# Hybrid flow backbone on one core: the scans' chunk blocks inverted by 32-row tiles, feature work and routing steps placed elsewhere

## The reference, cut to what matters

```python
def step(state, inp):                      # one token, per head; forward and backward in time
    r_t, w_t, k_t, v_t, a_t, b_t = inp
    sa = jnp.einsum('bhvk,bhk->bhv', state, a_t)
    state = (state * w_t[:, :, None, :] + sa[..., None] * b_t[:, :, None, :]
             + v_t[..., None] * k_t[:, :, None, :])
    return state, jnp.einsum('bhvk,bhk->bhv', state, r_t)
...
logits = (h @ w_router).astype(jnp.float32)
top_logit, top_idx = lax.top_k(logits, TOP_K)
```

## Time and profile before

| | us |
|---|---|
| median of 3 runs (lowest, highest) | 2844.2 (2843.36, 2848.82) |
| the profiled execution's own time | 2841.97 |
| its span | 2840.2 |
| PE, PEld busy | 2741.2, 2270.1 |
| DVE, ACT busy | 1923.5, 1524.9 |

### The profile page before, as it was taken

How to read it: one execution, slowest core, us unless ns; L and a number is a source line. 1 busy time by engine, 2 the same in 40 slices (tenths; PEclk the granted TensorE clock), 3 DMA queues, 4 the chain that set the end, 5 groups by cost and what they waited for, 6 DMA issues and landing times.

```text
span 2840.2 us, 49672 instructions
## 1 busy us (share of the span) xinstructions
PE 2741.2 (97%) x19396; PEld 2270.1 (80%) x19396; DVE 1923.5 (68%) x2524; ACT 1524.9 (54%) x2045; POOL 0.2 (0%) x4
## 2 busy tenths in 40 slices
PE   7999999999999999899999989999999999999997
PEld 5787777887788888667878988888888888888886
DVE  3766575336322333676656669888898988889897
ACT  5534374223322222543446447777777777777775
POOL 0000000000000000000000000000000000000000
PEclk8999999999999999999999989999999999999998
DMA  6010373224222232201034439999999999999995
GB/s 272 2 47 31 107 267 111 96 100 160 75 104 92 101 123 100 75 1 47 31 134 164 179 153 357 349 346 365 353 360 358 357 348 346 365 353 361 358 357 205
DMA packets 79842, 575.81 MB, mean 203 GB/s; under 512 B 8896, under 2 KB 10176, under 8 KB 10176
## 3 DMA queue, kind: packets, MB, share of 16 engines
q1 hardware_dynamic: 78960, 568.49, 53.1%
q10 hardware_dynamic: 720, 4.99, 0.4%
HBM read 572.39 MB, written 1.05 MB: 202 GB/s over the span
## 4 chain that ended last, share of the span: by engine, by line
PE 90%; DVE 6%; ACT 2%; issue 1%; DMA 0%; DVEq 0%; SPq 0%; ACTq 0%
PE bank L503 88%; ACT arena L1431 1%; PE bank L1339 1%; PE bank L1139 1%; DVE arena L2305 1%; DVE weights_low L1995 1%; DMA xT<-xin 0%; ACT weights_high L1431 0%; PE bank L924 0%; DVE arena L1971 0%; ACT hT L1431 0%; DVE arena L2211 0%; ACT L1431 0%; DVE arena L2091 0%; ACT modT L1431 0%
## 5 line engine op out<-in xcount | busy, mean ns | idle before, releaser
L1431 ACT ACTIVATE weights_high<-ring 128x1024 fp32r<-128x1024 f32 (+1 forms) x366 | 508.8, 1398 | 292.2 <-PE bank L503 291.9
L1431 ACT ACTIVATE arena<-bank 128x256 f32<-128x256 f32 (+7 forms) x581 | 255.6, 455 | 760.7 <-PE bank L503 684.1
L1995 DVE TENSOR_TENSOR weights_low<-ring,weights_high 128x1024 fp32r<-128x1024 f32 x220 | 266.7, 1224 | 403.0 <-ACT weights_high L1431 402.9
L2515 DVE TENSOR_TENSOR weights_low<-ring,weights_high 128x2048 fp32r<-128x2048 f32 x146 | 334.6, 2291 | 69.4 <-ACT weights_high L1431 67.9
L503 PE MATMUL bank<-h_low,weights_high 128*128 128x512 f32 (+1 forms) x960 | 346.8, 361 | 0.0
L503 PE MATMUL bank<-arena 64*64 64x64 f32 (+6 forms) x5168 | 301.2, 246 | 22.5 <-DVE arena L2211 5.8
L503 PEld LDWEIGHTS bank<-arena 64*64 64x64 f32 (+3 forms) x5168 | 252.1, 145 | 48.6 <-issue 17.4
L503 PE MATMUL bank<-weights_high,tokens_high 128*128 128x512 f32 x684 | 271.9, 397 | 1.6 <-DVEq L2538 1.6
L503 PE MATMUL bank<-weights_high,tokens_low 128*128 128x512 f32 x684 | 267.1, 390 | 0.0
L2515 DVE TENSOR_TENSOR more_weights_low<-arena,weights_high 128x2048 fp32r<-128x2048 f32 x108 | 247.4, 2291 | 25.0 <-ACT weights_high L1431 24.8
L1431 ACT ACTIVATE weights_high<-arena 128x2048 fp32r<-128x2048 f32 x108 | 207.0, 1917 | 47.1 <-PE bank L503 47.1
(11 more groups left out here) (294 smaller groups left out, 5348.0 us busy)
## 6 DMA issues: line engine op xcount, KB each, us to landing
ring<-wstream SPq DMA_DIRECT2D x372, 1024.0 KB, 4.8
arena<-wstream SPq DMA_DIRECT2D x167, 1024.0 KB, 4.8
sm<-small ACTq DMA_DIRECT2D x2, 1568.0 KB, 10.4
xT<-xin SPq DMA_DIRECT2D x1, 2048.0 KB, 9.8
cn<-consts ACTq DMA_DIRECT2D x1, 1636.0 KB, 6.6
out<-hT SPq DMA_DIRECT2D x2, 512.0 KB, 3.0
vec<-vecs SPq DMA_DIRECT2D x1, 121.5 KB, 2.6
cn<-consts ACTq DMA_DIRECT2D x1, 66.0 KB, 2.7
```

The lines of the kernel that those rows point to most:

```text
L1431: return nc.scalar.activation(o, i, func, **kw)
L1995: step(vx.tensor_tensor(ring_low[:, u % RING, cols], ring[:, u % RING, cols], wh[:, j % 4, :].bitcast(F32), ALU.subtract), "weights low", j)
L2515: return vx.tensor_tensor(low, raw, moe_high(q).bitcast(F32), ALU.subtract)
```

## The change

In the scans the doubling works on 32-row tiles. A helper `near` takes the place of `four`: for each head, four products of 32x32 by 32 columns, one per 32-row tile. E is cut in two: what lies in the same 32 rows but not in the same 16 (EB, mask "cross"), and what couples the two 32-row tiles of a half. F4 is the inverse at 16 rows, H = I + EB F4, and FT = F4 H the (transposed) inverse at 32 rows; Z is the coupling product that gives G1 at 64 rows. Z2, G2 and the second product of F4's kind are gone; D8 becomes a VectorE addition instead of a ScalarE copy; u is now the sum in PSUM of what u1 gave and the coupling. `gram_inner` issues 32 products instead of 16.

```diff
-            def four(o, left, right):
+            def near(b, at, left, right):
                 for h in range(4):
-                    for s in range(2):
-                        ins = mm(o[rows(s), h * HD:(h + 1) * HD], left[rows(s), h, :], right[rows(s), h, :])
+                    for t in range(4):
+                        ins = mm(bank[b][blk(t), at + h * BLK:at + (h + 1) * BLK], left[blk(t), h, :], right[blk(t), h, :])
...
             def carry_u(l, m):
+                pe.wait_ge(*done("G1", l, m))
...
-                        for s in range(2):
...
+                        for lead, follow in leads(groups[m][0]):
+                            ins = nc.tensor.matmul(bank[6 + p][blk(follow), P + q * HD:P + (q + 1) * HD],
+                                                   G_of[m % 2][blk(lead), 2 * p + q, follow % 2 * BLK:follow % 2 * BLK + BLK],
+                                                   u1[blk(lead), p, q, :], start=False, stop=True, skip_group_check=True)
...
# TensorE, solve(l, n), only the products of the solve
-                four(bank[4][:, 0:256], DD[:, 1], DD[:, 0])
-                four(bank[4][:, 256:512], DD[:, 0], DD[:, 1]).then_inc(*tick(products, "D2 product", l, n))
+                near(5, 0, DT, D)
+                near(5, P, D, DT).then_inc(*tick(products, "D2 product", l, n))
...
-                four(bank[4], DD[:, 1], DD[:, 0]).then_inc(*tick(products, "D8 product", l, n))
-                four(bank[5], DD[:, 0], FG[:, 0]).then_inc(*tick(products, "F3 product", l, n))
+                near(5, 0, D4[:, 0], D4[:, 1]).then_inc(*tick(products, "D8 product", l, n))
+                near(4, 256, D4[:, 1], F).then_inc(*tick(products, "F3 product", l, n))
...
-                four(bank[4][:, 256:512], D8, FG[:, 0]).then_inc(*tick(products, "F4 product", l, n))
+                near(4, 256, D8, F)
+                near(4, 384, F, D8).then_inc(*tick(products, "F4 product", l, n))
...
+                pe.wait_ge(*done("F4", l, n))
+                near(5, 0, E16, F4[:, 1]).then_inc(*tick(products, "H product", l, n))
                 if n:
                     carry_state(l, n - 1)
-                pe.wait_ge(*done("F4", l, n))
-                four(bank[5][:, 0:256], EC[:, 0], FG[:, 0])
-                four(bank[5][:, 256:512], FG[:, 0], EC[:, 0]).then_inc(*tick(products, "Z product", l, n))
-                pe.wait_ge(*done("masked k", l, n, 1))
-                across(bank[3], second, FG[:, 0], EC[:, 1], second).then_inc(*tick(products, "FC product", l, n))
+                pe.wait_ge(*done("H", l, n))
+                near(4, 256, F4[:, 0], H).then_inc(*tick(products, "FT product", l, n))
                 if n:
                     carry_y(l, n - 1)
-                pe.wait_ge(*done("Z", l, n))
+                pe.wait_ge(*done("FT", l, n))
+                pe.wait_ge(*done("masked k", l, n, 1))
+                for h in range(4):
+                    for t in range(second.start // BLK, second.stop // BLK):
+                        ins = mm(bank[3][blk(t), h * HD:(h + 1) * HD], FT[blk(t), h, :], EC[blk(t), 1, h, :])
...
-                four(bank[0], DD[:, 0], DD[:, 1]).then_inc(*tick(products, "Z2 product", l, n))
+                for h in range(4):
+                    for lead, follow in leads(d):
+                        at = 256 + h * HD + follow % 2 * BLK
+                        ins = mm(bank[0][blk(lead), at:at + BLK], E[blk(follow), h, :], FT[blk(follow), h, :])
...
# VectorE, solve(l, n)
-                    add(l, n - 1, 1, 0, 256, "G2")
...
+                elif n < 4:
+                    rates(l, 1, n - 2)
+                add(l, n, 4, "F2")
...
-                add(l, n, 0, 4, 256, "F4")
+                dve.wait_ge(*done("D8 product", l, n))
+                step(vx.tensor_tensor(D8, bank[5][:, 0:P].rearrange("p (h t) -> p h t", h=4), mask("eye32", BLK), ALU.add),
+                     "D8", l, n)
                 mask_k(l, n, 1)
+                if n in (0, 4):
+                    vx.memset(bank[0][:, 256:512], 0.0)
+                dve.wait_ge(*done("H product", l, n))
+                step(vx.tensor_tensor(H, bank[5][:, 0:P].rearrange("p (h t) -> p h t", h=4), mask("eye32", BLK), ALU.add),
+                     "H", l, n)
...
-                    rates(l, 1, n - 2)
-                    hats(l, 1, n - 2)
+                    second_hats(l, n - 2)
...
# ScalarE, solve(n)
+                    if n in (1, 2):
+                        second_exps(n - 1, 0)
+                        second_exps(n - 1, 1)
+                    if n in (1, 2):
+                        second_exps(n - 1, 2)
+                    copy(F4, bank[4][:, 256:512].rearrange("p (k h t) -> p k h t", k=2, h=4), ("F4", "F4 product"), n)
...
+                    if n == 0:
+                        f(es[:, 2:3], V("eps"), ACT.Exp)
...
-                    if n in (1, 2):
-                        exps(1, n - 1)
```

```diff
-                for t in range(2):
-                    ins = mm(bank[1 + 6 * t][:, 0:8], hT[:, k, CTX + t * P:CTX + (t + 1) * P], router_w[:, k, :],
-                             k == 0, k == KD - 1)
+                g = k % 4
+                ins = mm(bank[1][32 * g:32 * g + 32, 0:LAT], router_w[:, k, :], hT[:, k, CTX:TOK], k < 4, k >= 4)
...
# ScalarE, squares(...)
+                f(nm[:, 3:4], V("eps"), ACT.Sqrt)
                 for k in range(KD):
...
-                    if k == KD - 2:
-                        f(es[:, 3:4], V("eps"), ACT.Sqrt)
...
# ScalarE, layer 1, ahead of modulate
+                if l:
+                    first_high(0)
                 modulate(l, 2, both if l == 0 else both[1:], "ffn" if l == 0 else None)
...
# VectorE
+            dve.wait_ge(*done("first high", 0))
+            rest(0)
             dve.wait_ge(*done("logits"))
...
# VectorE, expert_pass, first instructions
+                dve.wait_ge(*in_pass(i - 1, "next high", AHEAD - 1))
+                rest(AHEAD - 1).then_inc(*tick(e_vectors, "low", AHEAD - 1))
```

More of the change, by code:

```diff
@@ L852, in gram_across @@
                 ins.then_inc(*tick(products, "gram across", l, n))
-            def last_power(l, n):
-                pe.wait_ge(*done("Z2", l, n))
-                pe.wait_ge(*done("G1", l, n))
-                four(bank[0][:, 256:512], D2[:, 1], FG_of[n % 2][:, 1]).then_inc(*tick(products, "G2 product", l, n))
             def across_second(l, n):
                 first, second = ends(groups[n][0])
-                pe.wait_ge(*done("G2", l, n))
+                pe.wait_ge(*done("G1", l, n))
                 pe.wait_ge(*done("FC", l, n))
-                across(bank[3], first, FW[:, 0], FG_of[n % 2][:, 1], second).then_inc(*tick(products, "W product", l, n))
+                across(bank[3], first, FW[:, 0], G_of[n % 2], second).then_inc(*tick(products, "W product", l, n))
             def solve(l, n):
@@ L1296, in _ @@
                 ins.then_inc(*tick(products, "tokens turned", i))
+                if i == 0:
+                    pe.wait_ge(*done("logit rows kept"))
+                    for t in range(2):
+                        ins = mm(bank[7][:, t * 8:(t + 1) * 8], T(LOGIT_ROWS)[:, t * P:(t + 1) * P], C("sel8", 8))
+                    ins.then_inc(*tick(products, "logits"))
             pe.wait_ge(*done("picks"))
@@ L1537, in _, with first_high @@
             act.dma_start(router_w[:], router).then_inc(router_loaded, 16)
+            def first_high(q):
+                act.wait_ge(moe_loaded[q], 16)
+                f(moe_high(q), moe_slot(q)[0], ACT.Copy).then_inc(*tick(scalars, "first high", q))
             for l in range(DEPTH):
@@ L1649, in solve @@
                     _, second = ends(groups[n][0])
-                    copy(D2, both_kinds(4), ("D2", "D2 product"), n)
+                    copy(D2, kinds(5), ("D2", "D2 product"), n)
                     if n:
@@ L1853, in _ @@
                             hidden_high(k)
-            for q in range(AHEAD):
-                act.wait_ge(moe_loaded[q], 16)
-                f(moe_high(q), moe_slot(q)[0], ACT.Copy).then_inc(*tick(scalars, "first high", q))
+            act.wait_ge(*done("logit rows"))
+            f(T(LOGIT_ROWS)[:, 0:LAT], bank[1][:, 0:LAT], ACT.Copy).then_inc(*tick(scalars, "logit rows kept"))
             for i in range(4):
@@ L1860, in _ @@
                     .then_inc(*tick(scalars, "tokens kept", i))
+            for q in range(1, AHEAD):
+                first_high(q)
             act.wait_ge(*done("top two"))
@@ L2126, in hat_k, with second_hats @@
                 step(vx.tensor_tensor(kh(d, j), X(d, KDIR_, j), X(d, TMP_, j), ALU.mult), "hats", l, d, j)
[L2128 to L2133 removed]
+            def second_hats(l, j):
+                dve.wait_ge(*done("exps", l, 1, j))
+                hat_a(1, j)
+                hat_b(l, 1, j)
+                hat_k(l, 1, j)
             def carry_u0(l, m):
@@ L2489, in _, with rest @@
                     weights_low(LAYER_START[1] + 2)
+            def rest(q):
+                raw, low = moe_slot(q)
```

(23 more changed lines are left out.)

174 lines of the change are left out of this document (105 added, 69 removed), and 3 rows, old and new, of the table _n.

## The result

The kernel after takes 2889.79 us (median of 4 runs, 2879.78 to 2892.62), the kernel before, on the same chip, 2843.78 (2843.13 to 2848.82): ratio 1.0152, 95% interval 1.0131 to 1.0172. I had forecast 2807, range 2793 to 2831.

What follows compares the result with a forecast made beforehand. TensorE's list was taken as the bound (PE busy 97%); scans -32.0, routing -1.1 and end -3.3 sum to -36.4 us, giving 2805.6 or 2807.8, forecast 2807; range 2794 to 2822, or 2793 to 2831 with the VectorE-order rival.

Steps and rivals of the forecast that it cites:

- Products, a round of four at 0.032 us: Scans: a round of four 32-row tiles takes columns plus 0.005 us, so new rounds cost 3.07, saving 2.55 us a group.
- the sum for a steady group, -2.55 +0.74 +0.3 -0.2: Scans, us per group: products -2.55, changes of tile form +0.74, F4's longer wait +0.3, D4's shorter wait -0.2; together -1.7.
- Rival A: Scans: 32-row tiles take turns; about equal at 2847 us (chance 0.05) or slower at 2862 (chance 0.05).
- B, the clock: Scans: clock falls to 1.2 GHz through both, some 10 us more in each of 16 groups, 2967 us; chance 0.03.
- the inner gram that I took at nothing: Scans: 64 records for 32, column time falls, starts double; bounds -0.2 and +0.4 us, taken as 0.
- Waits: Scans: F4's product waits 0.75 us for D8's addition instead of 0.33; D4's wait shrinks 0.2; H's addition hides behind state.
- Feature groups: Scans, dealt-out features: layer 0 groups 17.7 to 16.1 us; layer 1 20.30 to 14.6 (-5.7) and 18.14 to 15.1 (-3.0).
- The sign that was named, a clock of 1.00 in group 2: Layer 1's group 2: no wait over 1.5 us and a clock of 1.00 would show the forecast right.
- Routing: Router to gather: logits at about the same time, rank no longer behind `rest`, gather at 1689.75 against 1690.86; -1.1 us.
- The end: Kernel's end: an unused last `rest` goes and the Sqrt table load moves ahead; -2.3 -1.4 +0.4 = -3.3 us.
- The norms, put at 0: Other norms: the same move of the table load lies under TensorE's running products, so 0 us.

Runs made afterwards that it cites:

- split_64: `all_but_tiles` with each 64-column product of the inverse done as two of 32 columns, same weights and tile form; 2983.19 us.
- single_pass_near: The kernel after with each 32-row product taken from its operands' upper 16 bits, one record for two; 2849.44 us.
- single_64: `all_but_tiles` with each product of the inverse taken from its operands' upper 16 bits, one pass for two, in 64x64 tiles; 2800.25 us.
- merged: The kernel after with F2's product put into the records of one of D4's, 32 records a group fewer; 2863.22 us.
- all_but_tiles: `ends_and_routing` plus the second direction's features dealt out over groups, inverse still in 64-row blocks; 2826.84 us, ratio 0.9933 to the kernel before.
- ends_and_routing: The kernel before with the new routing, end, norms' table loads and gated writes, scans unchanged; 2836.39 us, ratio 0.9964.
- narrow stream: `all_but_tiles` with 512 extra 32-row, 32-column products on constants ahead of a wait in layer 0's group 1; the added run lasts 26.4 us.

## Why the prediction was wrong

*Products, a round of four at 0.032 us: the size was right.* H's `near` at 152.28 lasts 0.45 us with its last record's 0.2, so 32 records start in some 0.25: 0.031 a round. The basis was not: it took rounds to be held by their columns, and a round of two keeps its 0.057 with half of them (`split_64`), so that 0.032 came out is in part luck. There is a slip too: 0.46 us over 8 rounds is 0.0575, not 0.0585, 0.1 us a group.

*What failed is the sum for a steady group, -2.55 +0.74 +0.3 -0.2.* It added durations of records and never asked what hands them over. "11 `near`, each 32 records in 8 rounds" and the inner gram bring the group from 368 records to 604, and no term priced that; in the kernel after TensorE stands 31 times for want of instructions, 28.4 us in all. It also took the clock as 1.00 throughout, where 11 of 14 groups ran under 0.95. In before, 3 blocks need 10 us of 15.9, so nothing in that trace showed a limit. Rival A forecast a slower kernel (2862), for a reason that is not so: the tiles don't take turns.

*The rival that had part of it, B, the clock, had 0.03.* It asked for the low clock through all scans (+10 us a group); it came for part of the time. The time at 1.2 GHz is 105 us in the 14 windows, some 18 more behind the last ones. Equal groups tell its price: 20.31 against 16.53 us, less 1.9 for one stall more and longer ones, are 1.9 for 5.7 us (0.33); in `single_pass_near` 17.39 against 13.33, less 0.9, 3.2 for 8.3 (0.38). So an estimated 41 to 47 us for the 123 (the four runs of the kernel after, 40 us less at 1.2 GHz and 11 us shorter, give a lower price, 0.27, so the split is rough). The stalls are 28.4, and 31 times some 0.2 more that hides under the last record's modelled end: 34.6. Together 75 to 81 of the 90 that lie between the tiles' forecast (-27) and their result (+63), the larger part by the clock. The rest, 0.6 to 0.9 us a group, is open: the inner gram that I took at nothing (bound +0.4) is in it.

*The clock's own cause* is shown only so far: without stalls (single_pass_near), with 64-row tiles (single_64, split_64) and with next to no idle time (split_64, 0.3 us in a group of 30.7) it still falls; with fewer stalls in the same tiles (merged, one run) it fell less. What exactly it follows I can't say from these runs.

*Waits.* F4's product waits 0.71 (forecast 0.75), and H's addition hides behind state, as forecast.

*Feature groups: more than forecast.* Layer 1's group 2 gained 5.6 in `all_but_tiles`. The forecast's 5.7 held the tiles' 1.7, so 4.0 were the features'. Group 3 gained at last 2.0 (18.14 to 16.09), where they were to give 1.3; its missing part had been the loads. The sign that was named, a clock of 1.00 in group 2, came with the old tiles and not in the kernel after (0.61).

*Routing, -1.1 forecast, -3.3 measured* from the last product ahead of it to the first of the experts. The router starts 1.6 late (forecast 1.0), but the logits come sooner after it, and the ten rank products take 1.28 us where they took 2.14; the gather is 2.6 earlier, the first expert product another 0.8.

*The end, -3.3 forecast, -3.3 measured* from the first scattering product to the end of the span (22.8 us before, 19.5 after). The first addition starts 0.45 after the first scatter's last record does. All of the routing, the end and the norms gave some 10 us in `ends_and_routing` (6 to 14), against 4.4 forecast. The norms, put at 0, may be part of it: between the two scan stages the kernel after takes 1015.7 us, before 1019.2. The rest is open.

*Two rules that bear on it.* The Trainium skill, TensorEngine Tiling (Array Packing), Instruction Overhead, advises against tiles of a dimension that is already small. As advice it was right here; its reason, 60 cycles on each matmul, is not what the trace shows: within a block the narrow stream starts 128 records in 1.93 us less the last one's 0.2, 0.0135 each, even at 1.2 GHz. It would have given 2911, on the right side, but the stalls came from elsewhere. The failed step is the business of the Trainium skill, Runtime: NRT & Kernel Launch, Instruction fetch mechanics: instructions are refilled in blocks of 16 KiB, 256 instructions, and the cost of crossing a block is called mostly hidden, since instructions issue more slowly than they are fetched. The blocks agree with the trace (16 KB a packet, 128 records and their loads). The cover doesn't hold for TensorE here: in the narrow stream it stands 1.53 us at each block.

## What to carry to other kernels

Count TensorE's instructions beside their durations: here 256 of them, 128 fp32 records with their loads, cost about 3.46 us, so a stretch of some microseconds whose records average under 0.027 us is bound by supply, and cutting a product into smaller tiles then loses even if each tile is faster. Merge products that share weights before shrinking tiles, look for idle time on "issue" with large transfers beside it, and read a clock under 1.00 in a window as a cost of its own. And take a change apart: all of this one but the tiles was worth 0.67%, and the tiles cost over three times as much.

## What was not expected of the hardware

A block of TensorE's instructions takes some 3.46 us from start to start when nothing else holds it (five of six in the narrow stream), and three 1 MB transfers stretch it (stalls of 3.67 and 2.54 us). A round of two 64-row tiles takes 0.057 us with half its columns as with all. A reached wait is not free between small products: four of them cost up to 0.16 us, at a clock of 0.72.
